# DeltaNet's fronts begin beside RWKV's group norm; the inverses' results leave PSUM on two engines

## The reference, cut to what matters

```python
for l in range(DEPTH):                      # DEPTH = 2, x is (1, 256, 1024)
    p_a, p_b, p_c, p_g = _split(rms_norm(x, norm_mix[l]) @ w_in[l], ...)
    y_a, v_first = rwkv7_branch(p_a, ...)   # 16 heads of 64
    y_b = gated_deltanet_branch(p_b, ...)   # 8 heads of 128, chunks of 64
    y_c = dsa_mla_branch(p_c, ...)
    g_a, g_b, g_c = _split(sigmoid(p_g), 3)
    x = x + (g_a * y_a + g_b * y_b + g_c * y_c) @ w_mix_out[l]
    ...                                     # cross attention, FFN or 8 experts

# the end of rwkv7_branch: a group norm of each head, a gain, a bonus
mean, var = mean(o), mean(square(o - mean))
o = (o - mean) * rsqrt(var + RW_GN_EPS) * gn_g + gn_b + bonus

# the beginning of gated_deltanet_branch
qkv = silu(causal_dwconv(qkv, conv_w))
q, k = l2norm(q) * Dh ** -0.5, l2norm(k)
beta = sigmoid(b_in)
g = cumsum(-exp(A_log) * softplus(a_in + dt_bias))      # by chunk
decay = exp(where(incl, g_i - g_j, -inf))
Lmat = where(strict, (k * beta) @ k.T * decay, 0)        # then solved against (I + Lmat)
```

## Time and profile before

| | us |
|---|---|
| median of 3 runs | 2707.39 (2697.3 to 2718.16) |
| profiled execution, its own time | 2710.38 |
| its span in the profile | 2708.3 |
| mean granted clock of PE | 0.981 |
| layer 0's mixing stage, about | 100 to 560 |
| layer 1's mixing stage, about | 1064 to 1520 |

### The profile page before, as it was taken

One profiled execution on the slowest core, in us unless ns is written; L12 is line 12 of the kernel. 1 busy time (PEld: TensorE's weight loads), 2 busy tenths in 40 slices (PEclk: granted clock), 3 DMA queues, 4 the chain that ended last, 5 costly groups with the idle time before them and its releaser, 6 DMA issues.

```text
span 2708.3 us, 68645 instructions
## 1 busy us (share of the span) xinstructions
PE 2457.4 (91%) x30226; PEld 2037.1 (75%) x30234; DVE 1895.6 (70%) x2256; ACT 1599.8 (59%) x2162; POOL 367.0 (14%) x180
## 2 busy tenths in 40 slices
PE   6998999999999999989999999988988889898988
PEld 5866666778767777666667877778888888888887
DVE  5666664335455566676643354489999999999998
ACT  5454345333453344534443335478898888888886
POOL 0000001000000000000020000022343324233331
PEclk9999999999999999999999999999999999999999
DMA  6511221133446444311311334389999999999996
GB/s 205 163 49 49 64 63 41 48 117 109 140 152 217 160 148 121 94 49 33 94 32 41 116 110 131 135 307 386 383 389 384 386 386 388 384 387 385 383 389 231
DMA packets 304056, 531.43 MB, mean 196 GB/s; under 512 B 18544, under 2 KB 145776, under 8 KB 303376
## 3 DMA queue, kind: packets, MB, share of 16 engines
q1 hardware_dynamic: 303616, 525.99, 55.2%
q10 hardware_dynamic: 144, 1.05, 0.1%
HBM read 524.91 MB, written 2.10 MB: 195 GB/s over the span
## 4 chain that ended last, share of the span: by engine, by line
PE 50%; DVE 35%; ACT 8%; issue 6%; DMA 1%; POOLq 0%; POOL 0%; ACTq 0%; DVEq 0%; SPq 0%
DVE arena L3022 24%; PE bank L901 10%; PE bank L750 5%; PE bank L1424 4%; PE bank L1377 4%; PE bank L780 3%; PE bank L1440 2%; DVE yacc L3030 2%; PE bank L862 2%; PE bank L689 2%; PE bank L921 2%; PE bank L872 2%; PE bank L784 1%; PE bank L792 1%; PE bank L1157 1%
## 5 line engine op out<-in xcount | busy, mean ns | idle before, releaser
L3022 DVE TENSOR_TENSOR arena<-ring,arena 128x2048 bf16<-128x2048 f32 x334 | 830.7, 2531 | 1.9 <-ACT arena L2237 1.7
L2237 ACT ACTIVATE arena<-ring 128x2048 bf16<-128x2048 f32 x334 | 636.5, 1912 | 95.7 <-PE bank L1528 25.2
L1528 PE MATMUL bank<-arena 128*128 128x0 bf16 x10752 | 490.3, 209 | 102.4 <-DVE arena L3022 98.1
L1528 PEld LDWEIGHTS bank<-arena 128*128 128x128 bf16 x10752 | 478.3, 100 | 115.5 <-DVE arena L3022 105.6
L1678 POOL TENSOR_TENSOR arena<-yacc,arena 128x512 bf16<-128x512 f32 x112 | 309.8, 2778 | 945.5 <-ACT arena L2260 945.5
L901 PE MATMUL bank<-feat,ring 128*128 128x256 f32 x1408 | 366.0, 398 | 9.3 <-ACT arena L1740 4.2
L901 PEld LDWEIGHTS bank<-feat,ring 128*128 128x128 f32 x1408 | 256.8, 194 | 72.4 <-issue 26.2
L1545 PEld LDWEIGHTS bank<-arena 128*128 128x128 bf16 x5376 | 237.9, 98 | 19.7 <-issue 18.5
L1545 PE MATMUL bank<-arena 128*128 128x0 bf16 x5376 | 244.5, 206 | 5.1 <-issue 3.0
L1747 ACT ACTIVATE arena<-bank 128x256 f32<-128x256 f32 (+1 forms) x164 | 72.3, 441 | 210.2 <-PE bank L750 85.6
L1655 POOL TENSOR_TENSOR arena<-arena 64x512 f32<-64x512 f32 x16 | 22.4, 1402 | 1020.6 <-ACT arena L1887 859.9
(11 more groups left out here) (402 smaller groups left out, 3983.4 us busy)
## 6 DMA issues: line engine op xcount, KB each, us to landing
ring<-in_moe_w_gate SPq DMA_DIRECT2D x112, 1024.0 KB, 8.3
ring<-in_moe_w_up SPq DMA_DIRECT2D x112, 1024.0 KB, 7.7
ring<-in_moe_w_down SPq DMA_DIRECT2D x112, 1024.0 KB, 8.2
ring<-in_w_in SPq DMA_DIRECT2D x76, 1024.0 KB, 5.2
ring<-in_xa_w_kv SPq DMA_DIRECT2D x16, 1024.0 KB, 5.8
ring<-in_ffn_w_gate SPq DMA_DIRECT2D x11, 1024.0 KB, 5.4
ring<-in_ffn_w_up SPq DMA_DIRECT2D x11, 1024.0 KB, 6.0
ring<-in_ffn_w_down SPq DMA_DIRECT2D x11, 1024.0 KB, 5.9
```

The lines of the kernel that those rows point to most:

```text
L1528: m = mm(o, w[k // 4][wi][:, k % 4, col:col + P], xg[:, e % 2, xi, k, :].shape_from_register(width[e % 2]), start=i == 0 and k == 0, stop= ...
L2237: sc.activation(w_parts[b][0], ring[:, b * FFN_SLOT:(b + 1) * FFN_SLOT], ACT.Copy).then_inc(S["w_hi"], 1)
L3022: v.tensor_tensor(w_parts[b][1], ring[:, b * FFN_SLOT:(b + 1) * FFN_SLOT], w_parts[b][0], ALU.subtract).then_inc(S["w_lo"], 1)
```

## The change

It does six things. (1) The results of each inverse leave PSUM on ACT (the straight half) and DVE (the crossed half), and PE waits for both. (2) The last recurrence of `rwkv` takes three units of side work a step and not two, and the remaining eight stand in one piece behind the means; the filler shrinks from five matmuls to three, and PE no longer waits for the group norm's end before `gdn`. (3) On ACT the strengths and decays come before the norm's logarithms. (4) The sigmoids of RWKV's gate and of the strength become tangents, tanh(x/2), the gate's taken straight out of PSUM; DVE adds 1, and the factor one half comes in when the branches are merged. (5) The squares of a front are made one head ahead, the first two inside the group norm. (6) The last step of the group norm and RWKV's gating on DVE become a generator, `normed_and_gated`, of which a piece runs after every step of the first four fronts; the evacuation of DeltaNet's gate waits for the pieces whose input it overwrites. For room, two buffers move into `wl`.

```diff
-        gt = area(10, T)
+        gt = area(8, T)
-        kq = area(TT, 2, P)
-        dec = area(TT, P)
+        kq, dec = view(wl, 0, TT, 2, P), view(wl, 512, TT, P)
...
             yield left_over(l), True
-            yield 16, False
-            yield 16, True
+            yield 24, False
+            yield 8, True
...
                 pe.wait_ge(S["inv_XT"], c.need("inv_XT", len(sets)))
+                pe.wait_ge(S["inv_VX"], c.need("inv_VX", len(sets)))
...
-                filled(recur_rw(1), None, side, 2)
+                filled(recur_rw(1), None, side, 3)
                 for i in range(4):
                     mm(bk(GN_BANK[i]), C("blk"), branch[:, 2 * i:2 * i + 2, :], start=True, stop=True).then_inc(S["gn_m"], 1)
-                fill(side, 4)
+                fill(side, 8)
                 for i in range(4):
                     pe.wait_ge(S["gn_sq"], c.need("gn_sq"))
-                    mm(bk(GN_BANK[i]), C("blk"), tmp[:, 2 * i:2 * i + 2, :], start=True, stop=True).then_inc(S["gn_m"], 1)
-                    if i % 2:
-                        fill(side, 4)
-                fill(side, 4)
-                unread(5, 1)
-                pe.wait_ge(S["gn_y"], c.need("gn_y"))
+                    mm(bk(GN_BANK[i]), C("blk"), yacc[:, 2 * i:2 * i + 2, :], start=True, stop=True).then_inc(S["gn_m"], 1)
+                unread(3, 1)
...
                 for i, (nt, xt_, vu, w) in enumerate(sets):
                     act.wait_ge(S["inv_V"], c.need("inv_V"))
-                    straight, crossed = inv_halves(i)
+                    straight, _ = inv_halves(i)
                     for h, p_ in enumerate(HALF):
-                        sc.activation(xt_[p_, 0:2, p_], straight[p_, :, 64:P], ACT.Copy).then_inc(*c.inc("act_step"))
-                    for h, p_ in enumerate(HALF):
-                        sc.activation(xt_[p_, 2:4, p_], crossed[HALF[1 - h], :, 64:P], ACT.Copy).then_inc(*c.inc("inv_XT" if h else "act_step"))
+                        sc.activation(xt_[p_, 0:2, p_], straight[p_, :, 64:P], ACT.Copy).then_inc(*c.inc("inv_XT" if h else "act_step"))
...
+                    if free is not None and j % 2 == 0:
+                        act.wait_ge(S["gn_y"], free + j // 2)
-                    side_evac(dst[:, j, :], bk(banks[j], 0, T))
+                    side_evac(dst[:, j, :], bk(banks[j], 0, T), **kw)
...
-                yield from side_gates(gate_rw, 4, banks[25:])
+                yield from side_gates(gate_rw, 4, banks[25:], f=ACT.Tanh, scale=0.5)
...
+                sc.preload_act_table_set("silu_and_others")
                 for i, _ in enumerate(recur_rw(1)):
-                    fill(side, 2)
+                    fill(side, 3)
                     for n in SILU_AT[i]:
                         silu(l, n)
                 silu(l, 5)
                 c.skip("raw_free", 24)
+                strengths(l)
+                fill(side, 8)
                 sc.preload_act_table_set("natural_log_exp_and_others")
-                fill(side, 4)
+                decays(l)
                 for i in range(4):
-                    o = tmp[:, 2 * i:2 * i + 2, :]
+                    o = yacc[:, 2 * i:2 * i + 2, :]
                     act.wait_ge(S["gn_var"], c.need("gn_var"))
...
                     sc.activation(o, o, ACT.Exp, scale=-0.5).then_inc(*c.inc("gn_sd"))
-                    if i % 2:
-                        fill(side, 4)
-                fill(side, 4)
-                decays(l)
-                gates(gate_rw)
+                    if i < 2:
+                        squared(i, GD_BUFS[i])
...
+            def strengths(l):
...
+                sc.activation(b8[0:8, :], qkv[0:8, 26, 3:3 + T], ACT.Tanh, scale=0.5).then_inc(*c.inc("gd_ab"))
...
+            def squared(h, bufs):
+
                 act.wait_ge(*c.last())
-                sc.activation(b8[0:8, :], b_raw, ACT.Sigmoid).then_inc(*c.inc("gd_ab"))
-
-            def front_gd(l, heads, bufs):
+                sc.activation(bufs[0][:, 0:2, :], qkv[:, h:h + 9:8, 0:T], ACT.Square).then_inc(*c.inc("gd_sq"))
+
+            def front_gd(l, heads, bufs, after):
                 gt, kq, dec, (b_bc, b_ss, b_kk, b_tr) = bufs
-                for h in heads:
-                    act.wait_ge(*c.last())
-                    sc.activation(gt[:, 0:2, :], qkv[:, h:h + 9:8, 0:T], ACT.Square).then_inc(*c.inc("gd_sq"))
+                for h, later in zip(heads, heads[1:] + after):
                     act.wait_ge(S["gd_bc"], c.need("gd_bc"))
...
                     sc.activation(dec, dec, ACT.Exp).then_inc(*c.inc("gd_dec"))
+                    if later is not None:
+                        squared(later, bufs)
...
+                if before_last:
+                    yield 1
+                for i, (nt, xt_, vu, w) in enumerate(sets):
+                    _, crossed = inv_halves(i)
+                    dve.wait_ge(S["inv_V"], c.need("inv_V"))
+                    for h, p_ in enumerate(HALF):
+                        v.tensor_copy(xt_[p_, 2:4, p_], crossed[HALF[1 - h], :, 64:P]).then_inc(*c.inc("inv_VX" if h else "dve_step"))
+                        dve.wait_ge(*c.last())
...
+            def normed_and_gated(l):
+
                 for i in range(4):
                     o = branch[:, 2 * i:2 * i + 2, :]
                     dve.wait_ge(S["gn_sd"], c.need("gn_sd"))
-                    v.tensor_tensor(o, o, tmp[:, 2 * i:2 * i + 2, :], ALU.mult).then_inc(*c.inc("dve_step"))
+                    v.tensor_tensor(o, o, yacc[:, 2 * i:2 * i + 2, :], ALU.mult).then_inc(*c.inc("dve_step"))
...
+                    v.tensor_tensor(o, o, rkv[:, 8 + 2 * i:10 + 2 * i, :], ALU.add).then_inc(*c.inc("gn_y"))
+                    dve.wait_ge(*c.last())
+                    yield
...
+                    v.scalar_tensor_tensor(yacc[:, t, :], gate_rw[:, t, :], 1.0, branch[:, t, :], ALU.add, ALU.mult).then_inc(*c.inc("dve_step"))
+                    dve.wait_ge(*c.last())
+                    yield
...
             def gdn(l):
+                tail = normed_and_gated(l)
+                next(tail)
...
-                beside(front_gd(l, (0, 2), GD_BUFS[0]), front_gd(l, (1, 3), GD_BUFS[1]))
+                odd = front_gd(l, (1, 3), GD_BUFS[1])
+                for _ in front_gd(l, (0, 2), GD_BUFS[0]):
+                    next(odd, None)
+                    next(tail, None)
```

More of the change, by code:

```diff
@@ L1816, in values_beside, with side_gates @@
                     yield
-            def side_gates(dst, units, banks=(7,) * KT):
+            def side_gates(dst, units, banks=(7,) * KT, free=None, **kw):
                 for j in range(KT):
@@ L2052, in gdn @@
             def gdn(l):
-                sc.preload_act_table_set("natural_log_exp_and_others")
-                act.wait_ge(S["gd_g"], l + 1)
-                second = front_gd(l, range(4, 8), GD_BUFS[0])
-                side = gate_and_latent_beside()
-                both(front_gd(l, (0, 2), GD_BUFS[0]), front_gd(l, (1, 3), GD_BUFS[1]), side, FRONT_SIDE)
+                second = front_gd(l, (4, 5, 6, 7), GD_BUFS[0], (None,))
+                side = gate_and_latent_beside(l)
+                both(front_gd(l, (0, 2), GD_BUFS[0], (4,)), front_gd(l, (1, 3), GD_BUFS[1], (None,)), side, FRONT_SIDE)
                 act.wait_ge(S["gd_pool"], 8 * l + 4)
@@ L2465, in convs, with gated @@
                     yield
-            def gated(g, first):
+            def gated(g):
                 c.skip("proj_evac", KT)
@@ L2472, in gated, with inverted @@
                     dve.wait_ge(S["gate_sig"], c.need("gate_sig"))
[L2473 removed]
+                    v.tensor_tensor(branch[:, t, :], g[:, t, :], branch[:, t, :], ALU.mult).then_inc(*c.inc("dve_step"))
                     dve.wait_ge(*c.last())
[L2475 to L2479 removed]
+                    v.scalar_tensor_tensor(yacc[:, t, :], yacc[:, t, :], 0.5, branch[:, t, :], ALU.mult, ALU.add).then_inc(*c.inc("dve_step"))
+                    dve.wait_ge(*c.last())
+            def inverted(sets, corners=False, before_last=False):
                 q4 = lambda ap: ap.rearrange("p (a b) -> p a b", a=4)
@@ L2619, in rwkv @@
                         pass
-                    woven(inverted([rw_set(i, i) for i in range(2)]), b, conv, 0, skip=2)
+                    woven(inverted([rw_set(i, i) for i in range(2)], before_last=True), b, conv, 0, skip=2)
                     filled(inverted([rw_set(i, 2 + i) for i in range(2)]), None, conv, 1)
@@ L2720, in gdn @@
                 second = front_gd(l, range(4, 8), GD_BUFS[0])
-                beside(front_gd(l, (0, 2), GD_BUFS[0]), front_gd(l, (1, 3), GD_BUFS[1]))
+                odd = front_gd(l, (1, 3), GD_BUFS[1])
+                for _ in front_gd(l, (0, 2), GD_BUFS[0]):
+                    next(odd, None)
+                    next(tail, None)
+                for _ in odd:
+                    pass
+                for _ in tail:
+                    pass
                 v.memset(gXT[64:P, :, :, 0:64], 0.0).then_inc(*c.inc("dve_step"))
```

56 lines of the change are left out of this document (28 added, 28 removed).

## The result

The changed kernel takes 2697.35 us, the median of 20 runs (2696.32 to 2704.36). The kernel before, run beside it, took 2716.26, the median of 20 (2697.3 to 2721.74). The ratio of the runs is 0.9949, with a 95% interval of 0.9936 to 0.9962: half a per cent faster, where 0.83% was forecast. (It is not the quotient of the two medians, which is 0.993.) The profiled executions took 2696.57 and 2710.38 us, so 13.8 us are to be explained, and 22.6 were expected.

What follows compares the result with a forecast made beforehand. PE, busy 91%, sets the pace outside the experts, so only its waits and low clock in mixing can be won: -10.8 - 9.8 - 2.0 = -22.6, taking the median 2707.39 to 2684.8 us (-0.83%); range 2673 to 2703.

Steps and rivals of the forecast that it cites:

- Exits of the inverses: At ten inverse exits, splitting the copies between ACT and DVE saves 10.8 us, between 5 and 12.
- Filler: Between the last recurrence and the fronts, three filler matmuls instead of five save 1.8 us a layer.
- squares: In the DeltaNet fronts, PE's waits for ACT's squares go: 4.7 us saved a layer up to front 3.
- gap: In the first two pairs of fronts, PE newly waits for ACT's evacuation: +2.7 and +0.6 us a layer.
- handovers: In the last recurrence, four bank 7 handovers inside steps cost 0.47 us each: +1.9 us a layer.
- Norm tail on DVE: Norm groups and gate passes among the first four fronts: taken at nothing; 12 us if all lay bare.
- The stretched fronts: Rival: DVE's norm passes meet POOL in the fronts, up to 3 us a layer longer; 2696 us, chance 0.17.
- Clock: Fronts' old low-clock losses go, 7.1 us in layer 0, 5.3 in layer 1; new falls cost 2.6 a layer.
- Fronts 4 to 7: Late DeltaNet fronts: square waits of heads 5 and 7 go, 0.7 us each paid back; -2.0, between -5 and +1.
- the clock doesn't come back: Rival: from the first gap to front 3's end the clock stays at half, 27 us a layer; 2734, chance 0.06.
- the exits fail to pay: Rival: at the inverses' exits DVE is late or PE has another equally long wait; 2695 us, chance 0.06.
- the clock hold: Rival: no clock fall follows the new gap in the fronts, 2 x 2.6 us more won; 2679.6, chance 0.21.

Runs made afterwards that it cites:

- 1: Changed kernel with head 7's key scaling on DVE moved ahead of the exit copies in the first DeltaNet inverse; 2697.8 us, ratio to the kernel before 0.9941.
- 3: Kernel before with only the inverses' exits split, crossed copies on DVE and straight on ACT, head 7's key scaling behind them; 2705.15 us, ratio 0.9967.
- 6: Kernel before with the inverses' exits split between DVE and ACT, and head 7's key scaling ahead of the exit copies; 2701.23 us, ratio 0.9944.
- 8: Changed kernel with two units of side work a step in the last recurrence, 16 there and 16 behind the means; 2689.37 us, ratio 0.9913.
- 5: The kernel before, unchanged, profiled a second time; 2718.83 us, granted clock 0.977.

## Why the prediction was right in part and wrong in size

- **Exits of the inverses.** -10.8 forecast, -9.9 measured at the ten places; DVE's copy takes 0.29 us (0.3 taken). What failed is what was put at nothing, the exit of the first DeltaNet inverse, by the sentence that DVE is idle there "except in the first DeltaNet inverse, where PE didn't wait for L1800 anyway". It asked who waited for the copies that move, and not what stands behind them on the engine to which they move. That exit took back 2.1 us in layer 0 and 3.8 in layer 1 (1 and 3 show it; 6 gives 3.5 and 3.8 for it in the kernel before).
- **Filler, squares, gap, handovers.** Together -9.8 forecast and -11.0 measured. The first gap was 1.98 and 3.63 where 3.1 stood; the second 1.80 and 0.59 where 1 stood. In layer 0 the tile was out 28.4 us after the first mean matmul, forecast 28.3; the gap is shorter since the clock fell ahead of it and stretched the work that filled it (in the kernel of 1, where it didn't fall ahead of it, the gap is 3.63). From the first mean matmul to the end of front 3 it was 51.3 us in both layers, forecast 52. The handovers were 2.07 us against 1.9, but the prediction didn't see that two units a step would have been better (8).
- **Norm tail on DVE.** Taken at nothing, which held in the first pair and failed in the second of layer 0: a wait for bank 7 is 0.5 us there where ACT doesn't wait for DVE (8), and 1.80 where it does, so 1.3 us. The forecast put the second gap down to ACT's queue. The stretched fronts are partly true, and only in the second pair. DVE's passes of the same line and shape without POOL, and then beside it:

```profile
387.24 0.86 DVE L2667 TENSOR_SCALAR arena<-arena,par 128x256 f32<-128x256 f32 x2
388.13 0.69 DVE L2669 TENSOR_TENSOR arena<-arena 128x512 f32<-128x512 f32 x1
...
395.83 1.27 POOL L1661 TENSOR_TENSOR arena<-arena 128x256 f32<-128x256 f32 x1
396.54 1.43 DVE L2667 TENSOR_SCALAR arena<-arena,par 128x256 f32<-128x256 f32 x2
398.00 1.10 DVE L2669 TENSOR_TENSOR arena<-arena 128x512 f32<-128x512 f32 x1
```

  These are 1.0 of the 1.44 us for which ACT waits. The Trainium skill, page "SBUF — State Buffer", section "Who interferes with whom", names a DVE instruction with two SBUF inputs as one that contends with a GpSimd instruction that reads SBUF. `L2669` is of that kind and is stretched. `L2667`, with one tile and small operands, is stretched as well. The same section lists `tensor_scalar` among the operations that can take the shared ports in a mode of their own; no run here shows in which mode `L2667` ran.
- **Clock.** The falls after the first squares went, as forecast, and one short fall a layer came, of 1.7 us where 2.6 was taken. But the prediction took the clock elsewhere as fixed. It isn't (5): two executions of one kernel differ by 12 us of lacking clock and 8.4 us of time, and it took back the 6 us of experiment 1.
- **Fronts 4 to 7.** Here the failed step shows: -2.0 forecast (-5 to +1), +5.4 measured, 7.4 of the 8.8 us by which the forecast missed. The exit copies ahead of head 7's keys, put at nothing, add 2 x 2.07 and 1.69 of low clock. The squares ahead cost 0.67 us or a little more at each of three heads and give 0.96 at heads 5 and 7, about nothing a layer, where the forecast took a gain of 1.8 and a cost of 0.7 for each of two heads. The low clock behind head 5's gap in layer 0 went, 0.9 where 1.3 was taken.
- **Rivals.** That the clock doesn't come back didn't happen (a fall of 4 us, not of 27), nor did the exits fail to pay at their ten places; nor did the clock hold in either layer. The time lay in the range of 2673 to 2703, which was wide enough for the failed step.

## What to carry to other kernels

When an instruction moves to an idle engine, ask not only who waits for it but what stands behind it on its new engine, and who waits for that; an engine that is idle because it waits is not free. Where the gain is below 1%, follow the same instructions through both traces: a saving of 6 us was plain at its place and invisible at the end, where the trace shows more low clock behind it. Side work put into a loop costs a handover wherever a tile ends inside a step, so two units in every step were better than three.

## What the runs showed of the hardware

- One program on one core scatters by 25 us, 2696.5 to 2721.7. The runs for which the granted clock is given go with it: about 2698 us at 0.985 and 2716 at 0.976. The two traces of this program, at 0.981 and 0.977, have the same waits.
- The fall of the clock in the first pair of fronts has no fixed link to the idle time just ahead of it. In layer 0 of the changed kernel the granted clock is 0.57 from 380 to 384 us after a wait of 0.32; in the kernel of 1, the same program up to there, it is 1.00 after the same wait. Without the filler, after 2.89 us of standing still, the matmuls of 8 rows began at full clock (0.67 and 0.59 us, as with the filler), and the fall came in the work behind them.
- DVE and ACT copy 64x128 out of PSUM in nearly the same time, 0.29 and 0.27 us, while both do it at once.
